# A diagonal state space recurrence taken two tokens at a time, on VectorE and TensorE

## The chip, the cores and the metric

The kernel runs on one core of one Trainium2 chip (trn2). The time is that of one execution of the whole program on the device, in microseconds. The engines are TensorE (PE; its weight loads are shown as PEld), VectorE (DVE), ScalarE (ACT), GpSimd (POOL) and SyncE (SP), which here only issues the loads of weights.

## The reference

Two transformer blocks in float32 on 256 tokens of width 2048. The second block's odd layer is a block-diagonal state space layer (S5): 128 groups of 16 channels, each with 64 complex diagonal states. What it computes:

```
# h: (1, 256, 2048) after rms_norm; u = h as (1, 256, 128 groups, 16)
dt = exp(log_step)[:, None]
lb_re, lb_im = exp(dt*lam_re)*cos(dt*lam_im), exp(dt*lam_re)*sin(dt*lam_im)      # L, per group and state
cr, ci = (L - 1) / lam            # as real and imaginary part
bb = (cr + i ci) * (b_re + i b_im)                                               # B
bu_re, bu_im = einsum('blgh,gph->blgp', u, bb_re), einsum(..., bb_im)
s[t] = L * s[t-1] + bu[t]         # complex, an associative_scan over t in the reference
y = einsum('ghp,blgp->blgh', c_re, s_re) - einsum(..., c_im, s_im) + d_skip * u
y = gelu(y, approximate=False)
val, gate = split(y @ w_glu, 2)
return val * sigmoid(gate)
```

Before it stand a gated feed-forward layer (ffn0: norm, `w_ffn_in`, silu(gate) * up, `w_ffn_out`, norm, residual), behind it another (ffn1).

## The kernel before

**Layout.** Activations lie with channels on the 128 partitions: a tensor of width 2048 is 16 tiles (k) of 128 x 256 tokens. `res` is the residual stream. Matmuls of the large layers take weights in two parts, w_hi (a rounded copy made by ACT, function `hi`) and w_lo (the difference, made by DVE, `lo`), and activations in two parts (`act[:, k, 0:T]` by ACT, `act[:, k, T:]` by POOL, `act_low`).

**The weight stream.** SP loads w_raw in pieces of 512 KB, four (q = 0 to 3) to a pair i of output tiles; ACT's `hi`, then DVE's `lo`, then PE's `unit` (L1276), which takes two pieces. `split_pair` (L253) gives the order on ACT and DVE: `step(i, 3)`, `step(i + 1, 0)`, evacuation of the first tile, `step(i + 1, 1)`, `step(i + 1, 2)`, evacuation of the second. So three of four pieces of the next pair are staged ahead, also across the end of a phase. `run_phase` runs it, and its `behind` puts other work after each evacuation.

**ffn0.** Three groups of up gemm and down gemm (16, 16 and 12 tiles of hidden width). In the up gemm of the third group, `s5_behind(u)`, u counting units, prepares the S5 layer: L in `s5t` 11 and 12, `lam` for the scan, B in `b_dia` (two groups to a pair, block-diagonal in bands of 16 columns), turned by PE's transposes into `b_lhs` (L1317) and copied by ACT (L527). POOL adds up the down gemm's outputs and their squares (`square_sum`).

**S5.** A norm (`norm("s5", ...)`): ACT squares, PE sums over partitions, ACT takes the root, DVE the reciprocal and the scaled tiles `u5`. The state of a token is 128 partitions (two groups of 64 states) x 2 (real, imaginary) x 64 pairs of groups. The 256 tokens are four blocks tb of 64. For each block, `inputs(tb)` on PE (L1601) makes B u in banks m[0:4], 128 matmuls with 32 rows each; ACT copies them into `st0` or `st1` (L652); `scan` on DVE (L1088) goes token by token, in place, in three steps for each of two halves of the pairs: the product of lam and the previous state (L1097), and two additions (L1100, L1102). `outputs(tb)` on PE (L1614) makes C s in m[4] and m[5], 128 matmuls with 32 output columns. POOL multiplies u5 by d_skip in place (L1263), DVE adds the outputs to it (`y_add`, L1082). PE's order is inputs(0), inputs(1), outputs(0), inputs(2), outputs(1), inputs(3), outputs(2), outputs(3); DVE's is the scan of a block, then `y_add` of the block before it. After the last `y_add` come gelu (L656), the high parts (L358), the low parts (L1144) and the gemm glu. `c_raw` is loaded when ffn0's residual has been added; DVE spreads it into `c_lhs` (L1079).

**What is shared.** `st1` lies over `act`, `st0` over the upper part of the scratch; u5 serves as input, then as output. m has six banks of 2 KB, `bank` two, used by the gemms.

## Time and profile before

Median of three executions: 4095.63 us (4090.49 to 4099.43). The profiled execution took 4099.31 us; its span, from first to last instruction, is 4097.5 us, at a mean granted TensorE clock of 0.927.

| engine | busy us | share of the span |
|---|---|---|
| PE | 3656.4 | 89% |
| PE weight loads | 3149.2 | 77% |
| DVE | 2404.8 | 59% |
| ACT | 1969.5 | 48% |
| POOL | 712.5 | 17% |

The layer in question stands at these times of the trace (us from the span's start):

| stretch | from | to | us |
|---|---|---|---|
| down gemm of ffn0's third group, 15 of its 16 units | 2683.5 | 2746.5 | 63.0 |
| from the last residual addition of ffn0 to the first step of the scan | 2767.2 | 2814.3 | 47.1 |
| scan, first to last step | 2814.3 | 3091.3 | 277.0 |
| from there to the end of glu's second unit | 3091.3 | 3131.3 | 40.0 |

How to read it: busy times are of instructions, so PE's is an upper bound of its work, since matmuls overlap and their ends are modelled. The table by windows also gives the granted TensorE clock as a share of 2.4 GHz; 0.50 is the lower level of 1.2 GHz. In a timeline row, what stands in brackets is how long the engine was idle before the row and what released it.

### The profile page before, as it was taken

The page shows a single profiled execution, that of the slowest core. Times are in us where ns is not written, and L with a number is a line of the kernel's source. Part 1 is how long each engine was busy: PE and PEld are TensorE (multiplying, and loading weights), DVE is VectorE, ACT ScalarE, POOL GpSimd, SP SyncE. Part 2 cuts the span into 40 slices and gives each one's busy share as a digit, 9 for nine tenths or more (in the row PEclk, how much of TensorE's full clock was granted, in tenths as well). Part 3 has the DMA queues.
Part 4 walks back from the last instruction along what each step waited for, and adds up shares of the span by engine and source line. Part 5 has one row for each costly group of instructions (what it writes and reads, how often), then busy time and mean ns, then how long its engine had stood idle before and what let it go on. Part 6 is the DMA issues. An engine that isn't in the chain of part 4 may idle for free.

```text
span 4097.5 us, 64496 instructions
## 1 busy us (share of the span) xinstructions
PE 3656.4 (89%) x21616; PEld 3149.2 (77%) x21616; DVE 2404.8 (59%) x4056; ACT 1969.5 (48%) x2811; POOL 712.5 (17%) x835
## 2 busy tenths in 40 slices
PE   6999989999997899959899999985527989999997
PEld 5887768888886788748688888874426868888886
DVE  4665565555555455455655555776995565555556
ACT  3465444444444644434575444543114667545444
POOL 1000340011125310034300001070001130000107
PEclk9997999999998999979999999995658989999998
DMA  6560335555553555403355556560002535555555
GB/s 165 176 195 26 129 124 190 185 193 185 186 193 127 155 167 188 163 0 113 121 187 194 185 185 200 184 200 11 2 1 93 188 120 190 189 185 190 189 187 176
DMA packets 177283, 618.28 MB, mean 151 GB/s; under 512 B 18758, under 2 KB 29576, under 8 KB 176920
## 3 DMA queue, kind: packets, MB, share of 16 engines
q1 hardware_dynamic: 167424, 604.05, 45.9%
q10 hardware_dynamic: 9752, 12.81, 1.4%
q8 instruction: 66, 1.08, 0.1%
q14 instruction: 41, 0.34, 0.0%
HBM read 611.54 MB, written 5.24 MB: 151 GB/s over the span
## 4 chain that ended last, share of the span: by engine, by line
PE 81%; DVE 9%; POOL 5%; ACT 2%; issue 2%; ACTq 1%; DMA 0%; DVEq 0%; POOLq 0%
PE bank L1288 49%; PE bank L1291 26%; DVE prod L1097 3%; POOL act L1144 2%; POOL res L1149 2%; DVE st L1100 2%; DVE st L1102 2%; PE m L1337 1%; DVE rstd L701 1%; PE m L1576 0%; PE m L1550 0%; PE m L1415 0%; ACT w_hi L341 0%; ACT st L652 0%; PE m L1433 0%
## 5 line engine op out<-in xcount | busy, mean ns | idle before, releaser
L692 DVE TENSOR_TENSOR w_lo<-w_raw,w_hi 128x1024 fp32r<-128x1024 f32 x1148 | 1417.1, 1253 | 994.3 <-ACT w_hi L341 974.2
L1288 PE MATMUL bank<-act,w_hi 128*128 128x512 f32 x6528 | 1684.8, 398 | 46.4 <-POOL act L1144 40.5
L1288 PEld LDWEIGHTS bank<-act,w_hi 128*128 128x128 f32 x6528 | 1186.4, 191 | 297.9 <-POOL act L1144 49.7
L341 ACT ACTIVATE w_hi<-w_raw 128x1024 fp32r<-128x1024 f32 x1148 | 1189.4, 1054 | 401.2 <-PE bank L1291 394.5
L1291 PEld LDWEIGHTS bank<-act,w_lo 128*128 128x128 f32 x6528 | 899.2, 192 | 63.9
L1291 PE MATMUL bank<-act,w_lo 128*128 128x256 f32 x6528 | 918.3, 284 | 0.0
L345 ACT ACTIVATE low<-bank 128x256 f32<-128x256 f32 x572 | 218.8, 382 | 881.2 <-PE bank L1291 881.0
L1288 PE MATMUL bank<-ffn,w_hi 128*128 128x512 f32 x2432 | 612.1, 392 | 0.0
L1288 PEld LDWEIGHTS bank<-ffn,w_hi 128*128 128x128 f32 x2432 | 436.4, 189 | 77.2 <-POOL ffn L1186 0.2
L1186 POOL TENSOR_TENSOR ffn<-fv,ffn 128x256 f32 x152 | 113.6, 747 | 1498.3 <-ACT ffn L498 1097.7
L1291 PEld LDWEIGHTS bank<-ffn,w_lo 128*128 128x128 f32 x2432 | 333.9, 190 | 25.2
L1291 PE MATMUL bank<-ffn,w_lo 128*128 128x256 f32 x2432 | 341.5, 282 | 0.0
L696 DVE TENSOR_TENSOR ev<-bank,low 128x256 f32<-128x256 f32 (+1 forms) x404 | 170.2, 421 | 248.2 <-ACT low L345 248.2
L1627 PE MATMUL m<-st,c_lhs 128*32 128x64 f32 x1024 | 52.3, 388 | 166.2 <-DVE u L1086 129.5
L1627 PEld LDWEIGHTS m<-st,c_lhs 128*32 128x32 f32 x1024 | 48.3, 146 | 169.7 <-DVE st L1102 167.1
L1097 DVE TENSOR_TENSOR prod<-lam,st 128x128 f32<-128x128 f32 x510 | 139.3, 323 | 25.6 <-ACT st L652 25.6
L1199 POOL TENSOR_TENSOR y<-y,ev 128x256 f32 (+1 forms) x112 | 83.3, 743 | 356.9 <-DVE ev L696 354.4
L1164 POOL TENSOR_TENSOR sq<-y 128x256 f32<-128x256 f32 x96 | 97.0, 1010 | 266.3 <-DVE y L1120 156.1
L652 ACT ACTIVATE st<-m 128x512 f32<-128x512 f32 x64 | 58.4, 1065 | 150.3 <-PE m L1609 150.3
L1166 POOL TENSOR_TENSOR ssum<-ssum,sq 128x256 f32<-128x256 f32 x96 | 122.9, 1281 | 7.5
L1609 PE MATMUL m<-u,b_lhs 32*128 32x64 f32 x1024 | 81.6, 403 | 27.4 <-ACT st L652 18.5
L1609 PEld LDWEIGHTS m<-u,b_lhs 32*128 32x128 f32 x1024 | 71.5, 306 | 38.0 <-ACT st L652 28.1
(283 smaller groups left out, 2271.6 us busy)
## 6 DMA issues: line engine op xcount, KB each, us to landing
w_raw<-stream SPq DMA_DIRECT2D x1148, 512.0 KB, 3.4
toeplitz<-rel_rows ACTq DMA_DIRECT2D x1, 3072.0 KB, 32.5
res<-x_t ACTq DMA_DIRECT2D x4, 512.0 KB, 10.0
bias<-toeplitz ACTq DMA_DIRECT2D x1, 2048.0 KB, 10.6
out<-res SPq DMA_DIRECT2D x4, 512.0 KB, 2.8
bias<-toeplitz ACTq DMA_DIRECT2D x1, 1024.0 KB, 13.1
b_raw<-s_b ACTq DMA_DIRECT2D x1, 1024.0 KB, 7.1
c_raw<-s_c ACTq DMA_DIRECT2D x1, 1024.0 KB, 4.8
```

Of the source, the lines that this page charges most:

```text
L341: a(w_hi[:, q, :], w_raw[:, q, :], ACT.Copy).then_inc(hi_ready, 1)
L345: a(low[:, w, 0:n], bank[w][:, n:2 * n], ACT.Copy).then_inc(low_copied, 1)
L692: e.tensor_tensor(w_lo[:, q, :], w_raw[:, q, :], w_hi[:, q, :].bitcast(F32), ALU.subtract).then_inc(lo_ready, 1)
L696: e.tensor_tensor(dst, bank[w][:, 0:n], low[:, w, 0:n], ALU.add).then_inc(drained, 1)
L1097: ins = e.tensor_tensor(prod[:, h, :, :, :], lam[:, h, :, :, :], prev[:, :, g].unsqueeze(1).to_broadcast([P, 2, 2, 32]), ALU.mult)
L1164: e.tensor_tensor(sq[:, 2 * i + w, :], y[:, 2 * i + w, :], y[:, 2 * i + w, :], ALU.mult).then_inc(y_squares, 1)
L1166: e.tensor_tensor(ssum[:, :], ssum[:, :], sq[:, 2 * i + w, :], ALU.add).then_inc(y_squares, 1)
L1186: e.tensor_tensor(ffn[:, tile, T:2 * T], fv[:, w, :], ffn[:, tile, 0:T].bitcast(F32), ALU.subtract).then_inc(f_ready, 1)
L1288: mm(bank[w][:, 0:2 * n], w_hi[:, q, wt], x(h * hk + k, 0, 2 * n), start=(h == 0 and k == 0), stop=False)
L1291: last = mm(bank[w][:, n:2 * n], w_lo[:, q, wt], x(h * hk + k, 0, n), start=False, stop=(h == 1 and k == hk - 1))
L1609: last = mm(m[i][:, 128 * k + 64 * r:128 * k + 64 * r + 64], b_lhs[pr, r, 4 * bb + k, :], u5[pr, 4 * bb + k, 64 * tb:64 * tb + 64], start= ...
L1627: last = mm(m[4 + n][32 * i:32 * i + 32, 64 * k:64 * k + 64], c_lhs[:, r, pair, :], st[:, :, r, pair], start=(r == 0), stop=(r == 1))
```

## The change

The recurrence is written for pairs of tokens. With c for the pair, s[2c+1] = L^2 s[2c-1] + (L B) u[2c] + B u[2c+1]. The odd outputs are C s[2c+1] + D u[2c+1], the even ones (C L) s[2c-1] + (C B + D) u[2c].

- `lam` holds L^2, worked out at u = 14 of the up gemm. A second coefficient, L (cr + i ci), is worked out at u = 7, and a second matrix, `bl_dia` and `bl_lhs` for L B, beside `b_dia` and `b_lhs` for B. The one is made in the up gemm as before, the other in the down gemm of the third group, by `s5_behind_down` on DVE, PE and ACT, after a POOL memset of `b_dia` (128 x 4096). `alone` ends the last pair of that gemm without staging pieces of glu.
- `b_dia` and `b_lhs` now lie in `act`, `c_raw` and `cl_raw` in w_raw's place, `st1` (65 rows) over w_hi, w_lo and part of low. So c_raw is loaded by ACT's queue after the last `lo` of ffn0, and SP waits for `k_mm` and `c_done` before it loads glu's first four pieces; ACT and DVE make their high and low parts after the last outputs.
- PE makes K = the blocks of Re(C B) in m[4] (128 matmuls of 16 columns); DVE puts K + D into `k_lhs` and D into `d_dia`, and makes C L in `cl_raw` with six products and sums.
- `u5` is stored by parity. Inputs are two blocks b of 64 pairs, in eight banks by turns (`five_a`, `five_b`), with both matrices accumulated: 256 matmuls in a block. The order on PE is inputs(0), inputs(1), outputs(0), outputs(1).
- Outputs: 384 matmuls in a block; for each tile and parity the direct term (32 rows, 32 columns) starts an accumulation, two state terms (128 rows, 32 columns) end it. ACT's gelu reads the banks directly. `y_add` and the skip multiplication are gone.

```diff
+    st0 = at("st0", A, [P, 65, 2, 64])
+    st1 = at("st1", 64, [P, 65, 2, 64])
+    five_a, five_b = m[0:4], [bank[0], bank[1], m[4], m[5]]
 # SP
+        sp_eng.wait_ge(lo_ready, 4 * g0)
+        sp_eng.wait_ge(sem("k_mm"), 1)
+        sp_eng.wait_ge(sem("c_done"), 8)
+        for q in range(4):
+            load(g0, q)
 # ACT
+            for b in range(2):
+                st = (st0, st1)[b]
+                for rnd in range(4):
+                    for i in range(4):
+                        n = 16 * b + 4 * rnd + i
+                        s.wait_ge(sem("bu_mm"), n + 1)
+                        a(st[:, 1:65, :, 16 * rnd + i:16 * rnd + 16:4],
+                          (five_a, five_b)[rnd % 2][i][:, :].rearrange("p (k r t) -> p t r k", k=4, r=2),
+                          ACT.Copy).then_inc(sem("bu_cp"), 1)
...
+            for n in range(4):
+                gelu(0, n)
+            for n in range(3):
+                gelu(1, n)
+                glu_high(n)
+            gelu(1, 3)
+            hi(g0, 0)
+            glu_high(3)
+            hi(g0, 1)
+            hi(g0, 2)
 # DVE
+            if u == 14:
+                TT(8, t5(11), t5(11), ALU.mult)
+                TT(9, t5(12), t5(12), ALU.mult)
+                TT(8, t5(8), t5(9), ALU.subtract)
+                TT(9, t5(11), t5(12), ALU.mult)
...
+        def s5_behind_down(u):
+            if 1 <= u < 7:
+                bands(2 + (u - 1) // 3, (u - 1) % 3)
...
-            for tb in range(4):
-                st, prev = ((st0, st1), (st1, st0))[tb % 2]
-                v.wait_ge(sem("bu_cp"), 16 * tb + 16)
-                if tb:
-                    scan(st, 0, prev[:, 63, :, :], 3 * (64 * tb - 1))
-                for t in range(1, 64):
-                    scan(st, t, st[:, t - 1, :, :], 3 * (64 * tb + t - 1))
-                if tb:
-                    y_add(tb - 1)
-            y_add(3)
+            v.wait_ge(sem("bu_cp"), 16)
+            for c in range(1, 64):
+                scan(st0, 1 + c, st0[:, c, :, :], 3 * (c - 1))
+            v.wait_ge(sem("bu_cp"), 32)
+            scan(st1, 1, st0[:, 64, :, :], 3 * 63)
+            e.tensor_copy(st1[:, 0, :, :], st0[:, 64, :, :]).then_inc(sem("st_carry"), 1)
+            for c in range(1, 64):
+                scan(st1, 1 + c, st1[:, c, :, :], 3 * (63 + c))
+            for q in range(3):
+                lo(PH["glu"][0], q)
 # POOL
-            for tb in range(4):
-                g.wait_ge(sem("bu_mm"), 16 * tb + 16)
-                e.tensor_tensor(u5[:, :, 64 * tb:64 * tb + 64], u5[:, :, 64 * tb:64 * tb + 64],
-                                col("d_skip").unsqueeze(2).to_broadcast([P, DT, 64]), ALU.mult).then_inc(sem("y5_skip"), 1)
+            g.wait_ge(sem("bu_mm"), 32)
+            e.memset(cl_lhs[:, :, :, :], 0.0).then_inc(sem("s5_zero"), 1)
 # PE, inputs: for each tile kt and part r
+                            for j, lhs in ((0, bl_lhs), (1, b_lhs)):
+                                for i in range(4):
+                                    if k == 0 and r == 0 and j == 0:
+                                        if n >= 8:
+                                            pe.wait_ge(sem("bu_cp"), n - 8 + i + 1)
+                                        elif n == 4 and i == 2:
+                                            pe.wait_ge(sem("k_done"), 2)
+                                    pr = slice(32 * i, 32 * i + 32)
+                                    last = mm(dst[i][:, 128 * k + 64 * r:128 * k + 64 * r + 64], lhs[pr, r, kt, :],
+                                              u5[pr, kt, j, 64 * b:64 * b + 64], start=(j == 0), stop=(j == 1))
 # PE, outputs: for each tile kt
+                        for j, skip, lhs in ((0, k_lhs, cl_lhs), (1, d_dia, c_lhs)):
+                            for part in range(3):
+                                for i in range(4):
+                                    pr, pair = slice(32 * i, 32 * i + 32), 4 * kt + i
+                                    o = dst[n][pr, 128 * k + 64 * j:128 * k + 64 * j + 64]
+                                    if part == 0:
+                                        last = mm(o, skip[pr, kt, :], u5[pr, kt, j, 64 * b:64 * b + 64], start=True, stop=False)
+                                    else:
+                                        last = mm(o, lhs[:, part - 1, pair, :], st[:, j:j + 64, part - 1, pair],
+                                                  start=False, stop=(part == 2))
```

## Rows read from the trace of the kernel before

**Rows 1.** The profile page, part 1: busy us (share), instructions of each engine.

```profile
PE 3656.4 (89%) x21616; PEld 3149.2 (77%) x21616; DVE 2404.8 (59%) x4056; ACT 1969.5 (48%) x2811; POOL 712.5 (17%) x835
```

**Rows 2.** Table by windows: length; PE, PEld, DVE, ACT, POOL busy; clock, DMA, GB/s.

```profile
2683.46:2746.46 63.00, 63.00 (x363) 55.29 (x361) 45.71 (x47) 36.81 (x45) 57.70 (x45) 1.00 0.80 248
...
2767.24:2814.31 47.07, 32.03 (x294) 27.31 (x294) 10.84 (x21) 19.85 (x33) 5.45 (x3) 0.61 0.07 23
...
2814.31:3091.28 276.97, 98.26 (x1530) 87.99 (x1530) 276.97 (x1535) 45.35 (x49) 5.84 (x3) 0.58 0.00 1
...
3091.28:3131.28 40.00, 31.80 (x320) 24.95 (x321) 12.88 (x9) 16.29 (x28) 13.33 (x17) 0.72 0.12 34
```

**Rows 3.** Timeline of DVE: start us, busy us, engine, line, operation, tiles, count.

```profile
2822.84 0.48 DVE L1097 TENSOR_TENSOR prod<-lam,st 128x128 f32<-128x128 f32 x2
...
2823.78 0.48 DVE L1097 TENSOR_TENSOR prod<-lam,st 128x128 f32<-128x128 f32 x2
```

**Rows 4.** Groups by line, DVE, 2814 to 3092: busy us, mean ns, idle before.

```profile
L1086 DVE TENSOR_TENSOR u<-u,m 128x512 f32<-128x512 f32 x6 | 12.1, 2053 | 0.0
```

**Rows 5.** Table by windows of DVE line L1100 alone, while PE runs outputs.

```profile
2875.66:2887.48 11.82, 4.36 (x12) 0.91 0.01 3
...
2944.47:2959.67 15.20, 3.75 (x4) 0.94 0.01 2
```

**Rows 6.** Timeline of POOL and DVE: memset, skip multiplication, addition beside it.

```profile
2767.27 1.80 POOL L1259 MEMSET c_lhs<- 128x2048 f32 x1
...
2839.16 1.99 POOL L1263 TENSOR_TENSOR u<-u,cols 128x1024 f32<-128x1024 f32 x1 [26.14 <-PE m L1609]
...
2839.32 1.92 DVE L1100 TENSOR_TENSOR st<-st,prod 128x64 f32<-128x64 f32 x1
```

**Rows 7.** Timeline of PE: output bursts (L1627) and input bursts (L1609).

```profile
2800.43 3.67 PE L1609 MATMUL m<-u,b_lhs 32*128 32x64 f32 x58 [0.17 <-ACT st L652]
...
2875.79 11.69 PE L1627 MATMUL m<-st,c_lhs 128*32 128x64 f32 x256 [36.71 <-DVE st L1102]
...
2887.42 2.01 PE L1609 MATMUL m<-u,b_lhs 32*128 32x64 f32 x64
...
3092.02 12.64 PE L1627 MATMUL m<-st,c_lhs 128*32 128x64 f32 x256 [58.07 <-DVE u L1086]
```

**Rows 8.** Timeline of weight loads at changes of shape; durations of output matmuls.

```profile
2887.41 0.76 PEld L1609 LDWEIGHTS m<-u,b_lhs 32*128 32x128 f32 x24 [0.27 <-issue]
...
2959.60 1.19 PEld L1609 LDWEIGHTS m<-u,b_lhs 32*128 32x128 f32 x37 [0.42 <-issue]
...
L1627 PE MATMUL m<-st,c_lhs x1024: 277/387/580, 2875.8 to 3104.3; 128*32 128x64 f32 x171
```

**Rows 9.** Timeline of ACT: gelu before the gated gemm.

```profile
3105.45 3.89 ACT L656 ACTIVATE u<-u 128x1024 f32<-128x1024 f32 x4 [117.70 <-DVE u L1086]
```

**Rows 10.** Timeline in the down gemm: one weight piece through ACT, DVE, PE.

```profile
2690.08 1.07 ACT L341 ACTIVATE w_hi<-w_raw 128x1024 fp32r<-128x1024 f32 x1 [0.63 <-PE bank L1291]
...
2691.18 1.23 DVE L692 TENSOR_TENSOR w_lo<-w_raw,w_hi 128x1024 fp32r<-128x1024 f32 x1 [0.34 <-ACT w_hi L341]
...
2696.18 1.55 PE L1288 MATMUL bank<-ffn,w_hi 128*128 128x512 f32 x6
```

**Rows 11.** Timeline before the scan: square sums and scaling.

```profile
2768.10 9.12 PE L1337 MATMUL m<-u,ones 128*128 128x256 f32 x32 [17.44 <-ACT u L351]
...
2779.55 6.42 DVE L704 SCALAR_TENSOR_TENSOR u<-res,cols,rstd 128x256 f32<-128x256 f32 x16
```

**Rows 12.** The profile page, part 6: DMA issue, KB each, us to landing.

```profile
c_raw<-s_c ACTq DMA_DIRECT2D x1, 1024.0 KB, 4.8
```

**Rows 13.** Timeline in the up gemm: bands on DVE, transposes on PE.

```profile
2592.96 2.46 DVE L950 TENSOR_TENSOR b_dia<-b_raw,s5t 64x1024 f32<-64x1024 f32 x2
...
2599.01 2.90 DVE L952 TENSOR_TENSOR b_tmp<-b_raw,s5t 64x1024 f32<-64x1024 f32 x2
...
2643.52 0.46 PEld L1326 LDWEIGHTS m<-ident,b_dia 128*128 128x128 f32 x4
```

More of the change, by code:

```diff
@@ new lines, in _, with gelu @@
+            s.wait_ge(sem("s5_zero"), 2)
+            for r in range(2):
+                expand(r, c_lhs, c_raw, r)
+            s.wait_ge(sem("cl_ready"), 2)
+            s.wait_ge(sem("s5_zero"), 3)
+            for r in range(2):
+                expand(r, cl_lhs, cl_raw, r)
+            def gelu(b, n):
+                s.wait_ge(sem("y5_mm"), 4 * b + n + 1)
+                if b == 0 and n == 0:
+                    s.wait_ge(sem("y5_mm"), 4)
+                src = (five_a, five_b)[b][n]
+                a(y5[:, 4 * n:4 * n + 4, P * b:P * b + P].rearrange("p k (c j) -> p k j c", j=2),
+                  src[:, :].rearrange("p (k j c) -> p k j c", k=4, j=2), ACT.Gelu).then_inc(sem("y5_gelu"), 1)
@@ L1593, in _ @@
         if "s5" in plan:
-            if "ffn0" not in plan:
-                for u in range(24):
-                    s5_behind(u)
-            norm("s5", u5)
-            pe.wait_ge(sem("blhs_cp"), 8)
-            pe.wait_ge(scaled, SCALED["s5"] + DT)
-            def inputs(tb):
-                for bb in range(4):
+            pe.wait_ge(sem("c_loaded"), 16)
+            for kt in range(DT):
+                for r in range(2):
+                    for i in range(4):
+                        pair = 4 * kt + i
+                        last = mm(m[4][32 * i:32 * i + 32, T * r + 16 * kt:T * r + 16 * kt + 16], b_dia[:, r, pair, :],
+                                  c_raw[:, r, pair, :], start=True, stop=True)
@@ L1635, in _ @@
+            for b in range(2):
+                inputs(b)
+            for b in range(2):
+                outputs(b)
             gemm("glu", x_act, 16, act_tile("glu"))
```

294 lines of the change are left out of this document (167 added, 127 removed).

## The prediction, made before the result was known

> **What bounds the kernel now.** The page first: PE is busy for 89% of the span and DVE for 59% [rows 1], so an average says that this is a TensorE kernel. The table by stage says something else for the stretch that the change touches [rows 2]. In the 276.97 us of the recurrence (third row) DVE is busy for every one of them and PE for 98; in the 47.07 us before it and the 40.00 us after it no engine is full, which means a chain that goes from engine to engine. So the recurrence is bound by DVE, its two flanks by latency, and the last gemm before it (first row, 63.00 us) by PE, with POOL at 57.70 and DVE at 45.71 close behind.
>
> Next the timeline inside the recurrence. One token is three pairs of DVE instructions, and the same pair starts again 0.94 us later (2822.84 to 2823.78) [rows 3]; over the 63 steps of the first block but for one slow spot it is 0.947. 255 tokens at that pace are 241.5 us; the stretch is 276.97, so 35.4 us are something else. Six of the eight additions of L1086 fall in it, 12.1 us for DVE in all [rows 4]; two pairs of them stand between blocks and hold the scan up for 2.9 and 3.6 us, 6.5 together. The rest is slowness: while PE runs the 256 output matmul instructions of a block, DVE finishes 12 instructions of L1100 in 11.82 us (6 tokens where 12.5 fit: 6.1 us lost), then 4 in 15.20 (11.2 lost after the additions) [rows 5]; the third such time is like the first (6.7 lost). Once, POOL's skip multiplication and a DVE addition that should take 0.2 us stretch together to 1.99 and 1.92 us [rows 6]; three of these fall in the scan, 1.7 us each.
>
> **Term 1, the recurrence itself.** Before: 255 steps. After: 63 steps from the first block, one across, 63 more: 127, of the same shape, the squared transition being in lam. 127 x 0.947 = 120.3 us. The additions L1086 go (-6.5 us), so does the skip multiplication of POOL. In their place stand a copy of 0.2 us, and one memset of POOL (cl_lhs) in the first scan: between 0 and 3.6 us (the old memsets of half the size took 1.80 each [rows 6]); I take 1.8, nearest to what POOL's other instruction cost [rows 6]. Then the contention: output matmuls that read a state buffer were 768 instructions beside the scan, and are 512 (outputs(0)); outputs(1) stands behind it. st0 is read while DVE writes st1, as in the first and third case, 6.1 and 6.7 us for 256, so 12.8 us for 512; bounds 0 and 41, worked out below. Sum 120.3 + 0.2 + 1.8 + 12.8 = 135.1 us against 276.97: -141.9 us.
> The Trainium skill (SBUF — State Buffer, Who interferes with whom) says that only the port pair shared by VectorE and GpSimd causes contention and that PE never does; by it the 12.8 would be 0 and the time 13 us less. The trace here disagrees, with 6 and 2 tokens where 12 or more fit [rows 5].
>
> **Term 2, what stands behind the scan.** Before, 40.0 us from the last step to the end of glu's second unit (3131.28): 12.64 us of outputs [rows 7], additions, gelu, 16 copies, POOL's 16 low parts. After, outputs(1) has 384 matmuls, that is 768 instructions (each matmul is two in the trace: 128 per block are 256 there). 512 of them read strided states; the old ones went at 11.69/256 = 46 ns and 12.64/256 = 49 [rows 7]; I take 46: 23.6 us. The 256 for the direct terms read contiguous u5 like the inputs, which go at (2.01 - 0.4)/63 = 25 ns at the high clock and (3.67 - 0.4)/57 = 57 at the low one [rows 7]: 6.4 us, up to 14.6. Together 30 us.
> They also alternate in shape: a direct-term matmul uses 32 rows and 32 columns of the array, a state matmul 128 rows and 32 columns. Two changes for each of 16 x 2 groups are 64 in a block. The trace has two such changes of shape, output to input, and in front of both weight loading stands idle for 0.27 and 0.42 us with releaser "issue" [rows 8]. It may be the semaphore waits there (cost of a change: 0), or a pipeline that empties (cost up to a whole matmul, 387 ns, 25 us a block). I take 0.27: 64 x 0.27 = 17.3 us.
> The Trainium skill (TensorEngine Tiling (Array Packing), Key Properties) speaks for the second reading: it says that changing the tiling mode, not just the tile, drains TensorE. By it the 17 us are paid; by the first reading of the row they are not.
> Start 0.7 us, outputs 47.3, last gelu 0.5 (half of an instruction of 3.89/4 us [rows 9]), then the first weight piece, which could not be staged earlier since st1 lies over w_hi: 1.07 on ACT and 1.23 on DVE [rows 10], then two units of 16 tiles at 5.6 us (16/12 of the 4.2 in term 4): 62.0 us. Copies and low parts of the first 12 tiles are done by then, since four tiles come from PE every 12 us and POOL needs 3 for them. 62.0 - 40.0: +22 us; bounds +1 (25 ns for all, no price for a change) and +38.
> Outputs(0), 47 us, must fit beside the second scan of 73 us: it does, hidden. Gelu and the c expansions on ACT (8 instructions of about 1 us) and SP's four weight loads, now held until c_done, have the whole first scan of 60 us; nobody waits for them.
>
> **Term 3, what stands before the scan.** Before, 47.07 us [rows 2]: square sums on PE, 9.12 of them at a low clock in part, root and reciprocal 2.3, scaling 6.42 [rows 11], four rounds of 6.94 (3.67 of PE, then 3.6 of ACT's copies, one after the other), c_lhs. After, inputs are 512 instructions instead of 256 for the first block, but start with the first scaled tile, 6 us sooner, and have two sets of banks, so that copies lie beside matmuls. Round 0 takes 3.6 to 7.3 us; round 1 must wait for k_done, since K lies in m[4]: after the scaling DVE has two reductions, d_dia and four combinations, about 3 us, so at 18.4 us from the start. Three rounds then take 12 us (ACT's pace, warm clock) or 22 (57 ns), and the last copies 3.6. The six products for C L (7.5 us) are over at 27 and hidden. So 34.5 to 44: I take 38, since output bursts of 12 and 15 us have a mean granted clock of 0.91 and 0.94 [rows 5], so that they were at 0.5 for some 2 us and then at the high level, and these inputs are as long. -9 us; bounds -14 and +1.
> The 128 K matmuls (256 instructions at 25 to 57 ns, 6.4 to 14.6 us) wait for c_raw, now issued at 2747 and landing in 4.8 us [rows 12], and end at 2758 to 2767. The squares start at 2768.1: hidden by DVE's and POOL's residual work; if that cover failed, up to 5 us.
>
> **Term 4, the last gemm of ffn0.** The second matrix is prepared there: DVE gets six more pairs of 2.46 or 2.90 us [rows 13], 16.1 us. In that gemm DVE has (63.00 - 45.71)/15 = 1.15 us free in each unit of 4.2 [rows 2], 6.9 in six, so 9.2 are over. A piece of w_lo is done at 2692.41 and first read at 2696.18 [rows 10]: 3.8 us of lead absorb that much. 5.4 us remain. Then PE's own 8 groups of four transposes, 0.46 each [rows 13]: 3.7. Six more small products at u = 7 in the up gemm, about 0.5 after its slack. +9.5 us; bounds +4 and +18 (no lead, and POOL's memset of 3.6 in front of its queue, where POOL has 5 us to spare in 63 and DVE's bands wait for it).
>
> **Sum.** -141.9 + 22 - 9 + 9.5 = -119.4 us, say -120. The profiled execution took 4099.3 (1.8 more than its span of 4097.5), which becomes 3980; the median of before lies 3.7 lower, so 3976.
>
> **Rivals.**
> A: changes of shape are free, and instructions that alternate between column groups overlap better than the old order. For it: the 0.27 us also stand behind semaphore waits. Saves another 17 to 21: 3957.
> B: contention goes by time, not by instructions. Outputs(0) lasts 47 us, in which DVE has 0.51 tokens per us as in the first case [rows 5]: it loses 47 x 0.52 = 24 us, and at the second case's rate (2 tokens in 12.9 us) 41 us. 3988 to 4005. For it: both are the same traffic; against it: fewer state reads per us.
> C, the other side: alternating shapes in one accumulation serialise the outputs, so that each instruction takes its own full length. Place: outputs of both blocks; price 0.387 us [rows 8] x 768 = 297 us each, of which the second scan hides only 73: some 4480. It decides from 0.134 us an instruction, where 1536p = 120 + 30 + 56; seen are 25 to 57 ns, so it needs more than double. Against it: the order within a part steps through all four column groups.
> D, that the change does not do what it says: the steps do not shrink, as if waiting on copies: inputs(1) ends about 35 us into a scan of 60, so that bu_cp is early. No speedup at all would be 4096.
>
> **How the numbers follow.** Forecast 0.48 (its own range 3962 to 3992), A 0.25, B 0.22, C 0.03, D 0.02. Terms 3 and 4 move A down to 3945 and B up to 4008: that is the range. A measurement here tells 0.2% (8 us) from nothing. C is the slower part, D splits evenly between no change and a small gain.
>
> **What would show it.** Right: L1097's successor 254 times instead of 510, at 0.947 us a step; the recurrence at 130 to 140 us; outputs(1) at 44 to 50 us with PE weight loads idle 0.2 to 0.4 us at each change of shape; the gemm before 9 us longer with DVE near full. Wrong: outputs(1) below 32 us (A); second scan over 85 us (B); an output block beyond 100 us (C).

## The result, and the profile after

The changed kernel takes 3997.36 us (median of four executions, 3993.46 to 4000.28); the kernel before, beside it on the same chip, 4096.16. The ratio of the medians is 0.976, with a 95% interval of 0.9743 to 0.9777, so it is 2.4% faster. The forecast was 3976, its range 3945 to 4008; inside it the main line had 3962 to 3992 as its own range and rival B had 3988 to 4005. The profiled execution took 3996.6 us with a span of 3994.8: 102.7 us less than the span before.

The page, part 1, of the changed kernel (answers to [rows 1]): TensorE has 800 matmul instructions more (most matmuls are two in the trace), VectorE 743 instructions fewer.

```profile
PE 3673.4 (92%) x22416; PEld 3145.1 (79%) x22416; DVE 2299.8 (58%) x3313; ACT 1964.9 (49%) x2799; POOL 728.9 (18%) x833
```

The table by windows, with the columns of [rows 2], of the changed kernel. The stretches are the down gemm, the time from the last residual addition to the scan's first step, the scan, and the time behind it up to the end of the copy of glu's second unit.

```profile
2685.41:2766.00 80.59, 73.47 (x417) 63.90 (x416) 65.57 (x58) 39.47 (x53) 64.76 (x48) 0.98 0.56 176
2787.07:2824.15 37.08, 32.11 (x588) 31.16 (x587) 18.43 (x31) 15.46 (x18) 3.65 (x2) 0.56 0.01 2
2824.15:2972.30 148.15, 67.40 (x1216) 50.74 (x1214) 148.05 (x763) 26.61 (x29) 3.51 (x1) 0.65 0.04 16
2972.30:3030.90 58.60, 55.47 (x835) 37.06 (x836) 9.69 (x9) 28.44 (x33) 29.25 (x17) 0.97 0.15 48
```

Stretch by stretch, measured between the same instructions in both traces:

| stretch | before | after | difference | predicted |
|---|---|---|---|---|
| down gemm, all 16 units | 67.5 | 81.0 | +13.5 | +9.5 |
| before the scan | 47.1 | 37.1 | -10.0 | -9 |
| scan | 277.0 | 148.15 | -128.8 | -141.9 |
| behind the scan, to the copy of glu's second unit | 40.2 | 58.2 | +18.0 | +22 |
| sum | | | -107.3 | -119.4 |

The trace after had started the down gemm 6.2 us later. All of that was there some 1300 us earlier, in code that is the same in both kernels: such an offset is no part of the change. With it, the sum is -101, and the spans differ by 102.7.

**The scan.** The table by windows of DVE line L1194 (first addition of a step, two instructions a step) in the changed kernel: the first block, the second while TensorE runs outputs(0), and the rest of it.

```profile
2824.15:2883.97 59.82, 22.29 (x126) 0.50 0.10 37
2884.00:2927.40 43.40, 14.27 (x34) 0.96 0.01 2
2927.40:2972.30 44.90, 16.69 (x96) 0.55 0.00 0
```

63 steps in 59.82 us are 0.949 each, the forecast's pace. In the middle row 34 instructions, 17 steps, are done in 43.4 us, where 45.8 would fit. The second scan takes 88.3 us in place of the 60.8 that 64 steps and the copy need: 27.5 us are lost, not 12.8. The memset of POOL in the first scan cost about 0.2 us, not 1.8.

The timeline of DVE in that stretch (columns as in [rows 3]): pairs that took 0.35 and 0.48 undisturbed take 1.19 and 1.35 here, beside others that are as short as before.

```profile
2892.48 0.34 DVE L1194 TENSOR_TENSOR st<-st,prod 128x64 f32<-128x64 f32 x2
2892.73 1.19 DVE L1196 TENSOR_TENSOR st<-st,prod 128x64 f32<-128x64 f32 x2
2893.85 1.35 DVE L1191 TENSOR_TENSOR prod<-lam,st 128x128 f32<-128x128 f32 x2
2895.12 0.35 DVE L1194 TENSOR_TENSOR st<-st,prod 128x64 f32<-128x64 f32 x2
```

**Behind the scan.** The timeline of weight loads in outputs(1) of the changed kernel, two direct groups (L1747) and two state groups (L1749). A state load is the weight load of C or C L for a matmul that reads the state as its moving operand; the weights lie side by side, so its pace tells that of the matmul beside it.

```profile
2984.87 0.15 PEld L1747 LDWEIGHTS bank<-u,d_dia 32*32 32x32 f32 x8 [0.37 <-issue]
2985.11 0.66 PEld L1749 LDWEIGHTS bank<-st,c_lhs 128*32 128x32 f32 x16
2986.21 0.15 PEld L1747 LDWEIGHTS bank<-u,k_lhs 32*32 32x32 f32 x8 [0.44 <-issue]
2986.45 0.68 PEld L1749 LDWEIGHTS bank<-st,cl_lhs 128*32 128x32 f32 x16
```

In front of each direct group weight loading idles 0.37 to 0.44 us. From 2984.87 + 0.15 to 2985.11 there are 0.09 us more in front of the state group (0.17 where the clock is low, below). The block takes 43.5 us, most of its 32 pairs of groups 1.33 or 1.34 and those at the low clock up to 1.49.

### The profile page after: what moved, and what is told of

It reads as the page before. It is cut to its first block, busy times and chain, and to the rows that moved or that the text cites. A ratio compares the mean times of both kernels' runs of the same rounds, so it can differ in the third digit from the quotient of the medians.

```text
span 3994.8 us, 65185 instructions
## 1 busy us (share of the span) xinstructions
PE 3673.4 (92%) x22416; PEld 3145.1 (79%) x22416; DVE 2299.8 (58%) x3313; ACT 1964.9 (49%) x2799; POOL 728.9 (18%) x833
## 4 chain that ended last, share of the span: by engine, by line
PE 84%; DVE 7%; POOL 4%; issue 2%; ACT 2%; ACTq 1%; DMA 0%; DVEq 0%; POOLq 0%
PE bank L1378 50%; PE bank L1381 26%; POOL act L1238 2%; POOL res L1243 2%; DVE prod L1191 2%; DVE st L1194 1%; DVE st L1196 1%; PE m L1437 1%; DVE rstd L759 1%; DVE w_lo L750 0%; PE m L1722 0%; PE m L1676 0%; PE m L1650 0%; PE m L1749 0%; PE bank L1749 0%
## 5 line engine op out<-in xcount | busy, mean ns | idle before, releaser
L1292 POOL TENSOR_TENSOR y<-y,ev 128x256 f32 (+1 forms) x112 | 95.1, 849 | 366.4 <-DVE ev L754 365.9
L1259 POOL TENSOR_TENSOR ssum<-ssum,sq 128x256 f32<-128x256 f32 x96 | 113.2, 1179 | 7.5
L1437 PE MATMUL m<-sq,ones 128*128 128x256 f32 x160 | 56.5, 498 | 36.9 <-ACT sq L374 36.8
L521 ACT ACTIVATE ffn<-fv 128x256 f32 (+1 forms) x88 | 36.8, 418 | 105.6 <-DVE fv L927 105.6
L1243 POOL TENSOR_TENSOR res<-res,sq 128x256 f32<-128x256 f32 x96 | 82.7, 897 | 23.5 <-DVE sq L762 23.5
L1191 DVE TENSOR_TENSOR prod<-lam,st 128x128 f32<-128x128 f32 x254 | 75.6, 363 | 16.7 <-ACT st L682 16.7
L754 DVE TENSOR_TENSOR y<-bank,low 128x256 f32 x80 | 34.0, 425 | 85.2 <-ACT low L368 85.2
L1238 POOL TENSOR_TENSOR act<-sq,act 128x256 fp32r<-128x256 f32 x80 | 67.7, 883 | 82.0 <-ACT act L381 82.0
## 6 DMA issues: line engine op xcount, KB each, us to landing
bias<-toeplitz ACTq DMA_DIRECT2D x1, 1024.0 KB, 12.8
```

The source lines that it names most:

```text
L754: e.tensor_tensor(dst, bank[w][:, 0:n], low[:, w, 0:n], ALU.add).then_inc(drained, 1)
L1191: ins = e.tensor_tensor(prod[:, h, :, :, :], lam[:, h, :, :, :], prev[:, :, g].unsqueeze(1).to_broadcast([P, 2, 2, 32]), ALU.mult)
L1238: e.tensor_tensor(act[:, k, T:2 * T], src(k), act[:, k, 0:T].bitcast(F32), ALU.subtract).then_inc(act_ready, 1)
L1243: e.tensor_tensor(res[:, k, :], res[:, k, :], sq[:, k, :], ALU.add).then_inc(res_added, 1)
L1259: e.tensor_tensor(ssum[:, :], ssum[:, :], sq[:, 2 * i + w, :], ALU.add).then_inc(y_squares, 1)
L1437: last = mm(m[5][:, 0:T], ones[:, :], squares[:, k, :], start=(k == 0), stop=(k == kt - 1))
```

## The experiments

Twelve kernels. "The second scan" needs 60.8 us undisturbed, at 0.947 us a step. no_direct, late, contig, bridge and pad_st1 were executed once, the others four times or more. They ran on three chips and not beside the changed kernel; the kernel before took 4093.9, 4101.6 and 4102.0 us there. In these traces and the changed kernel's the last down gemm of ffn0 starts between 3.5 us before and 6.2 us behind that of the kernel before, and no edit of an experiment touches what comes ahead of it. So a difference of whole times against the 3997.36 can be off by some 10 us; the readings rest on stretches inside a trace.

### no_direct: the state terms alone

```diff
-                            for part in range(3):
+                            for part in (1, 2):
-    start=False, stop=(part == 2))
+    start=(part == 1), stop=(part == 2))
```

> The direct term (K and D from u) is left out of both output blocks, so half of what the outputs add up is missing; the state terms, all waits and all other work stay. The block outputs(0) should shrink from 43.4 us to 512 instructions of 44 ns, 22.7 us, without a change of shape. Theory T (DVE loses a fixed share of its pace, 0.63 of it, for as long as the outputs run): 14.4 us lost, the second scan takes 60.8 + 14.4 = 75 us. Rival S (each state instruction costs the scan a fixed amount, 27.5 us / 512 = 54 ns): the second scan stays at 88 us. Behind the scan outputs(1) falls from 43.5 to about 23 us by both, so the whole is some 34 us below the changed kernel by T and 21 by S.

Measured (3985.2 us, one execution), table by windows of all engines, then the timeline of DVE, both of this kernel:

```profile
2879.64:2909.30 29.66, 29.66 (x512) 28.45 (x512) 29.66 (x20) 0.00 (x0) 0.00 (x0) 0.94 0.01 2
...
2967.10:2996.70 29.60, 29.53 (x512) 28.21 (x512) 0.00 (x0) 21.58 (x7) 12.81 (x3) 0.92 0.01 2
```

```profile
2892.84 5.42 DVE L1191 TENSOR_TENSOR prod<-lam,st 128x128 f32<-128x128 f32 x2
2898.17 1.87 DVE L1194 TENSOR_TENSOR st<-st,prod 128x64 f32<-128x64 f32 x2
2899.97 2.52 DVE L1196 TENSOR_TENSOR st<-st,prod 128x64 f32<-128x64 f32 x2
2901.99 5.26 DVE L1191 TENSOR_TENSOR prod<-lam,st 128x128 f32<-128x128 f32 x2
```

DVE finishes 20 instructions in 29.66 us and nearly stands still, one step in 9.15 us where these rows stand. The whole scan takes 147.3 us, as before this edit: the loss is 27 us in a block of 29.7 us as in one of 43.4. That refutes theory T, which is the prediction's rival B: the loss does not go with time but with the state instructions, 512 of 54 ns. It also shows something nobody expected: without the direct groups a state instruction takes 58 ns, not 44. In the mixed order the changes of shape hide part of the slow reads (grouped2 below has the direct groups and shows it again).

### late: outputs(0) moved behind the scan

```diff
-                    pe.wait_ge(scan_step[h], 3 * (63 + 64 * b))
+                    pe.wait_ge(scan_step[h], 3 * 127)
```

> outputs(0) waits for the whole scan instead of its first block. All theories that put the slow stretch down to the outputs: the second scan takes 64 x 0.947 + 0.2 = 60.8 us instead of 88.3, and 43.5 us of outputs(0) move behind the scan: +16 us in all. Rival (the second scan is slow by itself, by its buffer or by what ACT and SP do then): it stays near 88 us, and the whole is 43 us longer.

Measured: 4012.27 us. L1194 by windows, first and second block:

```profile
2822.38:2882.15 59.77, 22.00 (x126) 0.50 0.10 37
2882.15:2942.80 60.65, 22.34 (x128) 0.50 0.00 0
```

The second scan is undisturbed, and the whole is 14.9 us above the changed kernel's median, 16 expected. So all 27.5 us come from outputs(0) running beside it, and hiding them there is still the better bargain. The two output blocks, now both behind the scan, take 85.9 us together, 42.9 each: with VectorE idle they are as slow as beside it.

### contig: neighbouring floats read

```diff
-    last = mm(o, lhs[:, part - 1, pair, :], st[:, j:j + 64, part - 1, pair],
+    last = mm(o, lhs[:, part - 1, pair, :], st[:, j + pair // 2, part - 1, 0:64],
```

> The state operand of the output matmuls is read from 64 neighbouring elements of the same buffer instead of one element of every 128 (the outputs are other numbers than the reference's); the count, shapes and order of the instructions stay. Theory P (it is the strided pattern that takes the buffer's bandwidth from DVE): the second scan falls from 88.3 to 61 to 65 us, and state weight loads go at 25 ns as the direct ones do instead of 44, so that outputs(1) falls from 43.5 to about 34 us; the whole 30 to 37 us below the changed kernel. Rival (any read of a partition by TensorE in that form costs DVE the same): the second scan stays near 88 us, or, if only the rate of reads counts, becomes 61 + 0.63 times the new length of outputs(0).

Measured: 3950.42 us. L1194 by windows while outputs(0) run, and the timeline of weight loads in them:

```profile
2875.20:2905.50 30.30, 11.10 (x64) 0.50 0.01 4
```

```profile
2890.46 0.20 PEld L1747 LDWEIGHTS m<-u,k_lhs 32*32 32x32 f32 x8 [0.17 <-issue]
2890.82 0.41 PEld L1749 LDWEIGHTS m<-st,cl_lhs 128*32 128x32 f32 x16 [0.17 <-issue]
```

32 steps in 30.3 us, 0.947 each: no loss at all, and outputs in 30.3 us. It is the pattern of the reads, not their number, that stops DVE. A state load takes 0.41/16 = 26 ns, and the 0.37 to 0.44 us in front of the direct groups are 0.17 here (0.21 in pad1, at the high clock): about half of that idle time goes with the slow reads. The granted clock is 0.50 in this row, 0.96 in the changed kernel's; pad1, at 0.94, shows that it is not the lower clock that spares DVE. This run does not tell yet whether the stride or its length matters.

### pad1: the stride kept, its length 516 bytes

```diff
-    st0 = at("st0", A, [P, 65, 2, 64])
-    st1 = at("st1", 64, [P, 65, 2, 64])
+    st0 = at("st0", A, [P, 65, 129])[:, :, 0:128].rearrange("p t (r g) -> p t r g", r=2)
+    st1 = at("st1", 64, [P, 65, 129])[:, :, 0:128].rearrange("p t (r g) -> p t r g", r=2)
```

> One float of padding after each token: the state of the next token lies 516 bytes on instead of 512; the access stays strided, one float per token. Theory N (neighbouring floats read together are what spares DVE): the stride of 516 bytes costs as 512 does, the second scan stays at 88 us and the output blocks at 43.5. Rival B2 (it is the power of two, by which all 64 reads of an instruction and DVE's accesses meet in the same part of the buffer): the second scan falls to 61 to 65 us, the outputs to 30 to 34, the whole about 35 us below the changed kernel.

Measured: 3952.49 us (3952.01 to 3955.68), ratio to the kernel before 0.964 (0.9621 to 0.9659). L1194 by windows while outputs(0) run, and weight loads in them:

```profile
2880.20:2908.90 28.70, 10.60 (x60) 0.94 0.02 4
```

```profile
2890.21 0.15 PEld L1747 LDWEIGHTS m<-u,d_dia 32*32 32x32 f32 x8 [0.21 <-issue]
2890.45 0.42 PEld L1749 LDWEIGHTS m<-st,c_lhs 128*32 128x32 f32 x16
```

One float of padding gives what contiguous reads gave: 30 steps in 28.7 us, a state load at 26 ns, outputs(1) 28.1 us. So rival B2's numbers come: 64 reads 512 bytes apart are slow and stop DVE; 516 bytes apart they go at 26 ns like neighbours. Its reason, that the addresses meet in one part of the buffer, is not shown: no other length of stride was tried for these reads, so whether it is the power of two or some other property of 512 stays open. The gain over the changed kernel, 44.9 us, is the 27.5 of the scan, 15.4 of outputs(1), and 2 more, which is within the offset of such traces.

The Trainium skill (SBUF — State Buffer, Door 1: The DMA port swizzle) holds that a read which crosses to a new 16-byte line pays a penalty, so that four-byte floats can be strided by 4 at most for free. Here a stride of 129 floats costs little or nothing against a stride of one: a state load takes 26 ns in both, at a clock of 1.00 here and 0.50 in contig; where the clock is still 0.50, at the start of outputs(0) here, it takes 27 to 28 ns. And the same page's Who interferes with whom, by which only the port shared by VectorE and GpSimd causes contention, is contradicted by these 27.5 us, which a padding of TensorE's operand takes away.

### inner2: the tokens innermost

```diff
-    st0 = at("st0", A, [P, 65, 2, 64])
+    st0 = at("st0", A, [P, 2, 64, 65])[:, :, :, :].rearrange("p r g t -> p t r g")
...
+                if b == 0 and n == 0:
+                    s.wait_ge(sem("st_carry"), 1)
```

(`st1` likewise.)

> The state buffers are laid out with the 64 tokens innermost, so that an output matmul reads 64 neighbouring floats and DVE's and ACT's accesses take the stride, 260 bytes; one wait more (the first gelu of block 0 on the carry copy). The whole computation is kept. Theory N, from the run with neighbouring floats read (no loss in the scan, outputs(1) 30 us): the loss of 27.5 us goes and outputs(1) is 13 us shorter, -40 in all, if a step of the scan stays at 0.947 us. Rival V (DVE pays for the stride that TensorE is rid of): each of the six instructions of a step is slower; from 0.32 us a step (40/127) on nothing is left of the gain, and beyond it the kernel is slower than the changed one.

Measured: 3999.36 us (3995.59 to 4002.79), the time of the changed kernel. The timeline of DVE in the first scan:

```profile
2840.87 0.69 DVE L1193 TENSOR_TENSOR prod<-lam,st 128x128 f32<-128x128 f32 x2
2841.49 0.43 DVE L1196 TENSOR_TENSOR st<-st,prod 128x64 f32<-128x64 f32 x2
2841.84 0.44 DVE L1198 TENSOR_TENSOR st<-st,prod 128x64 f32<-128x64 f32 x2
2842.19 0.67 DVE L1193 TENSOR_TENSOR prod<-lam,st 128x128 f32<-128x128 f32 x2
```

A step takes 1.32 us (2840.87 to 2842.19), and over the scan 1.29, where the break-even was at 0.947 + 0.32 = 1.27. Rival V holds: the stride was moved from the reader, half of which is hidden, to VectorE, which is the bound. The first and the second scan have the same pace, so the contention is gone here too; the slower step eats it.

### pad_st1: only the second buffer padded

```diff
-    st1 = at("st1", 64, [P, 65, 2, 64])
+    st1 = at("st1", 64, [P, 65, 129])[:, :, 0:128].rearrange("p t (r g) -> p t r g", r=2)
```

> Only the second state buffer has the stride of 516 bytes; outputs(0) still read the first one at 512 beside the second scan, which works in the padded buffer. Theory R (it is the reader's stride alone): the second scan stays at 88 us, outputs(1), which read the padded buffer, take 28.5 us instead of 43.5; the whole 15 us below the changed kernel. Rival M (it takes both, the reads' and DVE's addresses meeting in the same part of the buffer at every token): the second scan is well below 88 us too, and the whole is 30 to 42 us below.

Measured: 3976.09 us, 21 below the changed kernel where 15 were expected; its trace starts the down gemm 7 us earlier, ahead of any edit. L1194 by windows while outputs(0) read the unpadded buffer:

```profile
2877.00:2920.40 43.40, 19.60 (x33) 0.96 0.01 2
```

Like the changed kernel: 33 instructions in 43.4 us, the scan 148.25 us, and outputs(1), which read the padded buffer, take 28.3 us. Theory R, the reader's stride alone, holds in this kernel.

### before_pad0: the kernel before, its first buffer padded

```diff
-    c_lhs = at("c_lhs", A + 32, [P, 2, 64, 32])
-    st0 = at("st0", A, [P, 64, 2, 64])
+    c_lhs = at("c_lhs", A + 33, [P, 2, 64, 32])
+    st0 = at("st0", A, [P, 64, 129])[:, :, 0:128].rearrange("p t (r g) -> p t r g", r=2)
```

> The kernel before, its first state buffer alone with 516 bytes between tokens (there is no room to pad the second). By the reader's stride: the outputs of blocks 0 and 2, 6.1 and 6.7 us lost in the scan, cost nothing there any more and those of block 1, 11.2 us, as much as ever: 12.8 us less. By the rival that both buffers must be off the power of two: some other number, down to none.

Measured: 4076.32 us, ratio 0.9944 (0.993 to 0.9958): 23 us less, 17 to 29, where 12.8 were expected; the scan takes 253.9 us instead of 277.0. L1100 by windows while outputs of blocks 0, 1 and 2 run (answers to [rows 5]; `c_lhs` had to move up to make room):

```profile
2879.39:2887.16 7.77, 2.88 (x16) 0.87 0.02 5
2942.33:2953.82 11.49, 2.68 (x12) 0.83 0.01 3
3011.00:3018.80 7.80, 2.74 (x16) 0.78 0.02 5
```

Blocks 0 and 2, which read the padded buffer, lose nothing now (8 steps in 7.8 us), as theory R has it. But block 1, which reads the unpadded buffer while DVE works in the padded one, also got better: six steps in 11.49 us, of which some 3 are the additions, where two were done in 15.20. The stalls shrink from step to step there (1.59, 1.11, 0.60 us for the first three products). So what DVE touches counts too, in that kernel, though it did not in the run above. What the two buffers' places have to do with it, or the new place of `c_lhs`, stays open.

### grouped2: direct groups first in each bank

```diff
-                    for k in range(4):
+                    for stage, k in [(stage, k) for stage in range(2) for k in range(4)]:
-                            for part in range(3):
+                            for part in ((0,), (1, 2))[stage]:
-    last = mm(o, skip[pr, kt, :], u5[pr, kt, j, 64 * b:64 * b + 64], start=True, stop=False)
+    last = mm(o, skip[pr, kt, :], u5[pr, kt, j, 64 * b:64 * b + 64], start=(k + j == 0), stop=False)
...
-    start=False, stop=(part == 2))
+    start=False, stop=(k == 3 and j == 1 and part == 2))
```

> In each bank the eight direct groups come first and the state groups after them, 8 changes of shape a block instead of 64; the same instructions otherwise. Theory of the sum (a change costs the idle 0.17 and 0.38 us by itself, 17.6 us a block): outputs(1) takes 43.5 - 15.4 = 28 us, the whole is 15 us less. Rival R (state instructions that read strided floats take 58 ns each when nothing interrupts them, as in the run without direct terms, and the shape changes only hid that): 512 x 58 = 29.5 and 256 x 25 = 6.4 and 8 x 0.2: outputs(1) takes 37.5 us, the whole is 6 us less. The loss in the second scan stays at 27.5 us by both, as it goes with the state instructions.

Measured: 3990.09 us (3983.96 to 3996.83). Outputs(1) run from 2969.83 to 3005.4, 35.6 us: 7.9 less, near rival R's 37.5 and far from 28. State loads between others of their kind, timeline of weight loads:

```profile
2977.10 1.01 PEld L1749 LDWEIGHTS bank<-st,cl_lhs 128*32 128x32 f32 x16
2978.00 1.05 PEld L1749 LDWEIGHTS bank<-st,c_lhs 128*32 128x32 f32 x16
```

16 loads every 0.90 us are 56 ns each. The forecast's two terms, 17.3 us for changes of shape and 23.6 for state reads, were not independent: taking away 56 of 64 changes gives back about half of their price, since a state instruction then takes 56 to 58 ns again, as in no_direct. The scan still loses 27 us.

### spread: the bands two units apart

```diff
-            if 1 <= u < 7:
-                bands(2 + (u - 1) // 3, (u - 1) % 3)
+            if u <= 10 and u % 2 == 0:
+                bands(2 + u // 6, (u // 2) % 3)
```

> The six pairs of bands in the last down gemm come at units 0, 2, 4 ... 10 instead of 1 to 6. If the gemm is 13.5 us longer than before because DVE has more than a unit's work in six units in a row (6.37 us instead of 4.2), a unit with a band still takes 6.4 less what the lead and the free unit after it absorb (1.15 us of DVE's slack in it, and up to 3.8 us of lead once): the gemm falls from 81 to 72 to 75 us, the whole is 6 to 9 us less. Rival (the bands' time is paid wherever they stand, since TensorE waits for each piece): less than 2 us.

Measured: 3992.19 us (3988.2 to 3996.85). The down gemm takes 77.2 us instead of 80.9, so 3.7 less, between both expectations. Groups by line in this gemm: of the kernel before, of the changed kernel, of this one.

```profile
L1288 PE MATMUL bank<-ffn,w_hi 128*128 128x512 f32 x192 | 49.6, 393 | 0.0
L692 DVE TENSOR_TENSOR w_lo<-w_raw,w_hi 128x1024 fp32r<-128x1024 f32 x32 | 41.2, 1290 | 16.2 <-ACT w_hi L341 16.0
```

```profile
L1378 PE MATMUL bank<-ffn,w_hi 128*128 128x512 f32 x192 | 51.8, 406 | 7.1 <-DVE w_lo L750 7.1
L750 DVE TENSOR_TENSOR w_lo<-w_raw,w_hi 128x1024 fp32r<-128x1024 f32 x29 | 42.6, 1491 | 8.3 <-ACT w_hi L364 7.9
```

```profile
L1378 PE MATMUL bank<-ffn,w_hi 128*128 128x512 f32 x192 | 50.8, 400 | 3.5 <-DVE w_lo L750 3.5
L750 DVE TENSOR_TENSOR w_lo<-w_raw,w_hi 128x1024 fp32r<-128x1024 f32 x29 | 44.1, 1556 | 3.1 <-ACT w_hi L364 2.9
```

TensorE's idle time in front of w_hi falls from 7.1 to 3.5 us, 3.6 of the 3.7 us gained. But the mean of VectorE's w_lo grew from 1290 to 1491 ns with the bands, and to 1556 when they are spread. By the same view the splits are busy for 44.1 us, the 16 drains for 6.6 and the twelve bands for 17.6, 68 of 77 us, as much as the whole gemm took before (67.5): VectorE is nearly its bound now. Whether an order of the bands exists that comes nearer to 68 was not tried.

### bridge: no idle time in front of the inputs

```diff
             pe.wait_ge(sem("blhs_cp"), 16)
+            for n in range(6):
+                mm(bank[0][:, 0:T], ones[:, :], res[:, n, :], start=True, stop=True)
```

> Six matmuls of 128 x 128 by 256 (0.6 us each at the high clock, their result is overwritten) fill the 3 us in which TensorE is idle between the last square sum and the first scaled tile. Theory I (that idle time let the granted clock fall, and the inputs would keep it): the clock stays at 1.0 into the inputs, their 128 instructions of a round take about 3.5 us instead of 6.9, rounds 1 to 3 go at ACT's pace, and the stretch before the scan ends 6 to 9 us sooner. Rival F (matmuls of 32 rows do not hold the high clock, whatever came before): the clock falls to 0.5 within the first inputs although nothing is idle, the stretch is within 1 us of 37.1.

Measured: 3992.25 us, and the stretch no shorter. By windows, all engines: of the changed kernel the gap, round 0 of the inputs, and the rest of them; then round 0, the wait for K and the rest in this kernel.

```profile
2788.20:2791.20 3.00, 0.04 (x1) 0.02 (x1) 2.38 (x3) 0.47 (x1) 2.55 (x1) 1.00 0.00 0
2791.21:2798.10 6.89, 6.89 (x132) 6.78 (x132) 6.79 (x19) 0.39 (x1) 0.00 (x0) 0.55 0.01 2
2800.18:2848.00 47.82, 47.82 (x892) 47.82 (x892) 30.96 (x157) 23.43 (x27) 0.00 (x0) 0.50 0.01 3
```

```profile
2783.60:2787.50 3.90, 3.90 (x132) 3.87 (x132) 3.90 (x11) 0.09 (x1) 0.00 (x0) 1.00 0.02 4
2787.50:2792.30 4.80, 0.10 (x2) 0.00 (x0) 4.66 (x13) 3.59 (x4) 0.00 (x0) 0.88 0.00 0
2792.90:2840.00 47.10, 47.10 (x888) 47.10 (x890) 30.23 (x154) 22.04 (x24) 0.00 (x0) 0.50 0.01 3
```

Both theories were half right: rival F had the stretch, theory I what the idle time does. Round 0 keeps the full 2.4 GHz and takes 3.9 us instead of 6.9. But then TensorE waits 5.06 us for k_lhs instead of 2.00 (timeline of PE), the clock falls in that wait, and the other rounds stay at 1.2 GHz for 47 us in which TensorE is never idle. So no time is gained here, and a new question is put: would the inputs hold the high clock with neither gap?

### combo: padding, grouping and spreading together

> The changed kernel with 516 bytes between tokens, direct groups first in each bank, and the bands spread over units 0 to 10. If the three are independent: 45 us (padding), 56 changes of shape of 0.17 us each, 9.5 us (grouping, which with strided reads at 512 gave 7), and 3.7 us (the gemm with spread bands took 77.2 us instead of 80.9): 3997 - 58 = 3939 us. Rival: the shape changes are hidden in the padded outputs and grouping gives nothing: 3949.

Its edits are those of pad1, grouped2 and spread. Measured: 3942.0 us (3936.61 to 3944.75), ratio to the kernel before 0.9623 (0.9604 to 0.9642): 3 above the sum of the three, 7 below the rival, which whole times alone could not tell apart. The stretch can: outputs(1) take 22.1 us (2931.97 to 2954.1) instead of 28.1, so with fast reads a change of shape does cost its own time: 6.0 us less for 56 fewer, 0.11 each.

```profile
2775.50:2811.40 35.90, 31.09 (x584) 30.93 (x588) 18.42 (x31) 15.05 (x17) 2.39 (x1) 0.55 0.01 2
2811.40:2932.00 120.60, 45.36 (x1220) 43.43 (x1217) 120.43 (x763) 26.62 (x29) 3.51 (x1) 0.58 0.05 19
```

The scan, second row, is 120.6 us: 127 steps of 0.947 and a copy.

### combo_kb: and no gap before or inside the inputs

```diff
-            v.wait_ge(root_taken, n5 + 1)
-            e.reciprocal(rstd[:, :], rms[:, :]).then_inc(rstd_ready, 1)
...
+            v.wait_ge(scaled, SCALED["s5"])
             chain(e.tensor_reduce(eye32[:, :], ident[:, :].rearrange("p (a c) -> p c a", a=4), AX.X, ALU.add))
...
+            v.wait_ge(root_taken, n5 + 1)
+            e.reciprocal(rstd[:, :], rms[:, :]).then_inc(rstd_ready, 1)
```

All of VectorE's work on K, from eye32 to k_done, moves up from behind the scaling; with it come the edits of the combination and of bridge.

> As the combination, with the vectors of K computed in front of the wait for the norm's root, and the six filling matmuls in front of the inputs. Theory G (the clock falls in a gap of TensorE, and the wait for K is such a gap): rounds 0 and 1 both run at the high clock, in 3.5 us each, rounds 2 and 3 at the pace of ACT's copies, and the stretch before the scan falls from 37 us to 27 to 30: 3929 to 3932. Rival F2 (inputs of 32 rows lose the high clock after some us without any gap): only the wait for K goes, 2 us, and the stretch falls to 34 or 35.

Measured: 3925.97 us (3922.4 to 3928.45), ratio 0.9583 (0.9564 to 0.9602), 16.0 us below the combination. By windows, the stretch before the scan, then the scan, then the inputs of the first and of the second block alone:

```profile
2775.90:2799.20 23.30, 22.34 (x662) 20.98 (x665) 17.69 (x28) 15.60 (x18) 3.65 (x2) 1.00 0.01 3
2799.20:2919.80 120.60, 33.03 (x1157) 30.64 (x1155) 120.47 (x763) 26.47 (x29) 3.51 (x1) 0.64 0.06 19
2780.50:2799.20 18.70, 18.61 (x646) 18.34 (x650) 13.17 (x21) 14.73 (x16) 0.00 (x0) 1.00 0.01 4
2799.20:2810.60 11.40, 11.25 (x386) 10.97 (x382) 11.39 (x73) 11.35 (x13) 0.08 (x1) 1.00 0.02 4
```

Theory G holds, and more than it promised: with no gap over 0.9 us all four rounds are at 2.4 GHz (clock 1.00 in the first row). The stretch takes 23.4 us from the last residual addition on, in place of 37.3 (the combination's window above begins 1.3 us behind that addition). The same matmuls of 32 rows that did not leave 1.2 GHz in 48 us without a gap once they were there hold 2.4 GHz for 30 us, both blocks of them, when they begin there. Moving K alone, without the filling matmuls, was not run. This is the fastest kernel of the study, 4.2% below the one before.

## Why the prediction was right, and where it was not

**The whole.** The measured 3997.4 lies in the stated range, but outside the main line's own 3962 to 3992 and inside rival B's 3988 to 4005, and B's sign, a second scan over 85 us, came as well (88.3). The forecast's way and its pace of a step were right; that the range held is owed to the room it gave to B, whose reason is wrong. Of the 21 us missed, the four terms are 12.1, the offset of this trace 6.2.

**The steps of the scan** were right: 127 of them at 0.949 and 0.947 us, half of the old number, at the old pace. That is the whole gain, and everything else is what it cost.

**The contention term** was the one mis-sized: 12.8 us forecast, 27.5 measured. Within the changed kernel it does go with the number of state instructions, as the forecast took it: the run without direct terms showed 27 us for the same 512 in a block a third shorter. The size was not right. [Rows 5] offered 6.1 us for 256 instructions and 11.2, and the forecast took the smaller case because buffer and writer seemed to correspond. Twice the larger is 22.4, nearer to 27.5. Per instruction that is 24 and 44 ns before and 54 now, so the number is not all: in the second case before, the 256 instructions took 15.20 us, 59 ns each, which is the pace of no_direct. What decides between the cases stays open. In the kernel before, the forecast had counted 24.0 us lost beside the three output blocks in the scan; padding one buffer gave 23 of them back. Rival B, at 24 to 41 us of loss, had the number inside it and a wrong reason.

**Behind the scan** +18 instead of +22. Changes of shape have a price, as the forecast chose against rival A: some 0.09 + 0.42 us of idle weight loading in each of 32 groups, 16 us, 17.3 forecast. The rest of the difference is the matmuls themselves, 43.5 us for the block instead of 47.3. Yet the price was not separate from the reads' (7.9 us came back for 56 of 64, and 6.0 with padded buffers). The Trainium skill (TensorEngine Tiling (Array Packing), Key Properties) says that a change of tiling mode drains the array; the padded kernel's idle 0.21 us in front of each direct group agrees.

**Before the scan** -10 for -9, by luck: two errors cancelled. The forecast had the inputs at the high clock after some 2 us; they stayed at 0.50 for all four rounds but their first microsecond, and rounds 1 to 3 with their copies took 24.0 us where the warm case had 15.6. And it had overlooked that squares and square sums now run tile by tile beside POOL's residual additions, because ACT no longer waits for the whole residual. The timeline of PE, the last square sums of the changed kernel, behind which the last residual addition ends at 2787.0:

```profile
2786.86 1.38 PE L1437 MATMUL m<-u_sq,ones 128*128 128x256 f32 x4 [0.17 <-ACT u_sq L374]
```

They end 1.2 us behind that addition; before, they ended 10.0 us behind it [rows 11]. So nearly 9 of the 10 us come from an overlap that the forecast did not have, and the inputs gave 1. The wait for K came as the forecast had it, 2.0 us of TensorE's time, and ended 13.1 us into the stretch, 18.4 in the forecast.

**The down gemm** +13.5 for +9.5. The twelve bands took 17.3 us of VectorE (16.1 forecast) and the transposes 4.8 of TensorE (3.7). The slack was counted with w_lo at 1290 ns, and beside the bands it takes 1491: 29 of them are 5.8 us more. The other three of the 32 are glu's, which the change moved behind the scan. TensorE, which had no idle time in front of w_hi, now has 7.1 us there, where the forecast left 5.4 over. w_hi's own matmuls took 2.2 us longer, 51.8 instead of 49.6.

**Rivals C and D** did not come: the output block took 43.5 us for 768 instructions, 57 ns each, where C's price was 387, and inputs(1) were done long before the second scan.

## What to carry to other kernels

Before counting contention as a tax on hidden work, look at the reader's stride: where one matmul reads one float per 512 bytes, pad the row by one float and measure again (other lengths were not tried); here that was worth 45 us, against 99 for the whole change. When a serial chain is halved, what was hidden beside it is not halved with it: list what now stands behind the chain (43.5 us of outputs), what is slower beside it, and price each from the worst row that you have, not from the one that looks most alike. And a stage between two idle times of TensorE may stand at half clock throughout: close both gaps; here the first alone gave nothing, and both together 14 us.

## What the hardware showed that was not expected

- State reads of TensorE 512 bytes apart: 58 ns a weight load and matmul when nothing is between, with VectorE at one step in 9.15 us instead of 0.947; with VectorE idle the blocks are no faster (42.9 us each in late). At 516 bytes, or side by side: 26 ns, and VectorE undisturbed.
- Matmuls of 32 rows did not raise the clock from 1.2 GHz (48 us without a gap at 0.50, in the changed kernel) and did not lose 2.4 GHz (30 us at 1.00, in combo_kb). The outputs, whose state matmuls have 128 rows, went from 0.50 to 1.00 in their first microseconds at both strides of the state, but stayed at 0.50 for 30 us when they read neighbouring floats, at the same 26 ns a load. Why is open; no run here separates it.
- A change of tile shape costs 0.17 us of weight loading each way at the low clock and 0.21 and 0.09 at the high one, and 0.37 to 0.44 where slow reads end.
- VectorE's weight split took 1290 ns on average in the down gemm before and 1491 to 1556 with the bands between the splits, though the splits are the same instructions. In each of the three traces the two splits with no addition or product of POOL beside them take 1.22 us, and every split over 1.25 us, up to 1.76, has one beside it, though not every split beside one is slow. So it may be that the bands only move the splits against POOL's work; no run took POOL's work away to show it.
